# Sums of squares of a recurrence: one fp32 matmul for each half against two fp32r matmuls on high and low parts

## The reference, cut to what matters

```python
qkv_a = jax.nn.silu(causal_conv(qkv_a, conv_w)).astype(jnp.float32)
q_a = qkv_a[..., :GDN_WIDTH].reshape(b, s, GDN_HEADS, GDN_HEAD_DIM)       # 16 heads of 128
k_a = qkv_a[..., GDN_WIDTH:2 * GDN_WIDTH].reshape(b, s, GDN_HEADS, GDN_HEAD_DIM)

def l2norm(x):
    return x * lax.rsqrt(jnp.sum(x * x, axis=-1, keepdims=True) + L2_EPS)
q_a = l2norm(q_a) * (GDN_HEAD_DIM ** -0.5)
k_a = l2norm(k_a)
o_a = gated_delta_rule(q_a, k_a, v_a, g, beta)
```

## Time and profile before

| | |
|---|---|
| median of 3 runs | 3941.32 us (3936.63 to 3944.15) |
| span of the profiled execution | 3936.2 us |
| TensorE matmul / weight load busy | 96% / 91% of the span |
| VectorE busy | 71% |
| ScalarE busy | 48% |
| mean granted TensorE clock | 0.992 |

### The profile page before, as it was taken

How to read it: one execution, slowest core, us unless ns; L and a number is a source line. 1 busy time by engine, 2 the same in 40 slices (tenths; PEclk the granted TensorE clock), 3 DMA queues, 4 the chain that set the end, 5 groups by cost and what they waited for, 6 DMA issues and landing times.

```text
span 3936.2 us, 73085 instructions
## 1 busy us (share of the span) xinstructions
PE 3791.8 (96%) x28822; PEld 3598.6 (91%) x28822; DVE 2786.2 (71%) x3780; ACT 1888.4 (48%) x2849; POOL 185.9 (5%) x188
## 2 busy tenths in 40 slices
PE   1999999999999999999999999999999999999998
PEld 1999999999999999999999999999988798989888
DVE  7788887757777778888675675565576666666676
ACT  1546455335544355555533554454565433334365
POOL 0111211000000012121000000000000000000000
PEclk8999999999999999999999999999999999999999
DMA  9533433863368843434385434445534445555543
GB/s 396 182 141 138 143 135 141 304 220 142 140 236 311 297 148 139 144 138 147 139 317 198 140 140 169 182 162 179 187 111 168 171 171 193 182 183 183 182 149 129
DMA packets 137169, 716.41 MB, mean 182 GB/s; under 512 B 37184, under 2 KB 37632, under 8 KB 60800
## 3 DMA queue, kind: packets, MB, share of 16 engines
q1 hardware_dynamic: 111456, 631.31, 44.6%
q10 hardware_dynamic: 25504, 82.13, 5.9%
HBM read 711.22 MB, written 2.16 MB: 181 GB/s over the span
## 4 chain that ended last, share of the span: by engine, by line
PE 84%; DVE 7%; ACT 4%; issue 3%; DMA 2%; DVEq 0%; ACTq 0%; SPq 0%
PE bank L278 17%; PE bank L280 17%; PE bank L279 17%; PE bank L295 8%; PE bank L296 4%; PE bank L2346 2%; PE bank L2348 2%; PE bank L317 2%; PE bank L2347 2%; ACT Wh L343 2%; PE bank L321 2%; DMA raw<-in_ada 1%; DVE Wl L349 1%; PE bank L319 1%; PE bank L320 1%
## 5 line engine op out<-in xcount | busy, mean ns | idle before, releaser
L343 ACT CAST Wh<-raw 128x1024 fp32r<-128x1024 f32 x1124 | 1169.1, 1047 | 1664.1 <-PE bank L280 1226.0
L349 DVE TENSOR_TENSOR Wl<-raw,Wh 128x1024 fp32r<-128x1024 f32 x1124 | 1383.0, 1235 | 788.9 <-ACT Wh L343 784.1
L278 PE MATMUL bank<-H,Wh 128*128 128x256 f32 x5440 | 1597.0, 294 | 2.0 <-DVE Wl L349 1.2
L279 PE MATMUL bank<-H,Wh 128*128 128x256 f32 x5440 | 1538.4, 283 | 0.0
L280 PE MATMUL bank<-H,Wl 128*128 128x256 f32 x5440 | 1538.0, 283 | 0.0
L278 PEld LDWEIGHTS bank<-H,Wh 128*128 128x128 f32 x5440 | 1041.9, 192 | 29.2 <-issue 17.5
L279 PEld LDWEIGHTS bank<-H,Wh 128*128 128x128 f32 x5440 | 1042.5, 192 | 11.3 <-issue 8.6
L280 PEld LDWEIGHTS bank<-H,Wl 128*128 128x128 f32 x5440 | 1041.5, 191 | 0.0
L295 PE MATMUL bank<-H,Wh 128*128 128x512 f32 x1280 | 449.9, 396 | 6.4 <-DVE WS L336 6.1
L296 PE MATMUL bank<-H,Wl 128*128 128x256 f32 x1280 | 358.6, 280 | 0.0
L295 PEld LDWEIGHTS bank<-H,Wh 128*128 128x128 f32 x1280 | 240.6, 188 | 66.2 <-issue 5.5
(11 more groups left out here) (413 smaller groups left out, 4776.7 us busy)
## 6 DMA issues: line engine op xcount, KB each, us to landing
raw<-in_stream SPq DMA_DIRECT2D x560, 1024.0 KB, 4.8
WS<-in_ada ACTq DMA_DIRECT2D x94, 512.0 KB, 6.1
raw<-in_ada SPq DMA_DIRECT2D x32, 1024.0 KB, 7.6
gm_more<-in_ada ACTq DMA_DIRECT2D x20, 512.0 KB, 6.9
WS<-rows_d ACTq DMA_DIRECT2D x16, 512.0 KB, 5.2
KR<-in_ada ACTq DMA_DIRECT2D x14, 512.0 KB, 6.9
raw<-in_stream SPq DMA_DIRECT2D x8, 512.0 KB, 6.8
X<-in_x_t SPq DMA_DIRECT2D x1, 2048.0 KB, 17.0
```

The costliest lines, as they stand in the source:

```text
L278: pe.matmul(out[:, 0:T], wh, xh[:, kt, :], start=first, stop=False)
L279: pe.matmul(out[:, 0:T], wh, xl[:, kt, :], start=False, stop=False)
L343: act.copy(Wh[:, n % 4, :], raw[:, (sbk + 2) % 4, k * (D // 2):(k + 1) * (D // 2)]).then_inc(hi_ready, 1)
L349: dve.tensor_tensor(Wl[:, n % 4, :], raw[:, (sbk + 2) % 4, k * (D // 2):(k + 1) * (D // 2)], Wh[:, n % 4, :].bitcast(F32), ALU.subtract).t ...
```

## The change

```diff
+        ones_r = sb("ones_r", [P, P], F32R)
...
+        sq_hi, sq_lo = ([O[:, at + h, :, :] for h in range(2)] for at in (KT - 2, KT - 4))
...
             S.done(act.activation(ROPE[:, 1, :], rx[:, 3, :], ACT.Sin), "act", "sin")
+            S.done(act.copy(ones_r[:], ones), "act", "ones_r")
...
                 if n == (SCAN + 4 if chain else SCAN + 3):
-                    F.wait(pe, "act", "sq", f)
+                    if not chain:
+                        st_setup.wait(pe, "act", "ones_r")
+                    F.wait(pe, "dve", "sq_lo1", f)
                     for h in range(2):
-                        m = pe.matmul(B[h][:, :], ones, tm2[:, 2 * h:2 * h + 2, :], start=True, stop=True)
+                        pe.matmul(B[h][:, :], ones_r[:], sq_hi[h], start=True, stop=False)
+                        m = pe.matmul(B[h][:, :], ones_r[:], sq_lo[h], start=False, stop=True)
                     F.done(m, "pe", "ssq")
...
                 if n == (SCAN + 3 if chain else SCAN + 2):
                     F.wait(act, "dve", "silu", f)
+                    for h in range(2):
+                        F.done(act.activation(sq_hi[h], cs2[:, 2 * h:2 * h + 2, :], ACT.Square), "act", f"sq_hi{h}")
                     F.done(act.activation(tm2, cs2, ACT.Square), "act", "sq")
...
+                if fresh and n == (SCAN + 4 if chain else SCAN + 3):
+                    F.wait(dve, "act", "sq", f)
+                    for h in range(2):
+                        F.done(dve.tensor_tensor(sq_lo[h], tm2[:, 2 * h:2 * h + 2, :], sq_hi[h].bitcast(F32), ALU.subtract), "dve", f"sq_lo{h}")
                 if n or not chain:
                     late = 1 if chain else 0
                     dve_low(dve, q + (n - late) // 8, (n - late) // 2 % 4, (n - late) % 2)
```

## The result

The changed kernel takes 3950.03 us (median of 20 runs, 3944.02 to 3955.99), the kernel before 3944.49 us beside it (20 runs, 3936.63 to 3950.11). The ratio is 1.0014, with a 95% interval of 1.0007 to 1.0020: slower by 5.5 us (2.8 to 7.9), and within 0.2%. The forecast was +6.0 us, 3947.3, with a range of 3938 to 3954. It held, though it was put on a median of 3941.3 and the one measured here is 3944.5, and its terms are off by more than the sum shows.

A forecast was written before the change was run, and what follows sets the result against it. The prediction took TensorE's stream and its waits to bound the kernel. Gains of 4.6 us beside chains, losses of 7.6 in first pairs and 3.0 for the clock gave +6.0 on 3941.3: 3947.3 us, range 3938 to 3954.

The forecast's parts named there:

- What is removed and added on TensorE: Sums in each front: two fp32 matmuls (1.72 us) become four fp32r (0.92 us), 0.80 us less to stream.
- The wait beside a chain: In the 14 fronts beside a chain, TensorE waits 0.47 us for VectorE's subtractions before the sums.
- The 14 gains: Each front beside a chain gains 0.80 - 0.47 = 0.33 us, 4.6 us for 14.
- What hides the rest: Beside a chain, idle time on ScalarE (0.51 us) and VectorE (0.75 us) absorbs the delay, so "qkn" moves forward with TensorE.
- The rival that it gives the gain back: At the next chain TensorE waits for "qkn", losing the 14 fronts' gain: +8.8 to +10.6 us, 3951; chance 0.12.
- The wait in the first pairs: In each layer's first pair, without a chain, sums start 4.6 us later; each loses 3.8 us, both 7.6.
- The clock: After each first pair's long wait, TensorE's clock is low for 3.4 us, costing 1.5 us each, 3.0 in all.
- the case of 6.8 us: Rival: the low clock lasts twice as long in both first pairs, +9.0 us, 3950.3; chance 0.09.
- The sum: Whole kernel: -4.6 + 7.6 + 3.0 = +6.0 us, 3947.3 from a median of 3941.3.

The follow-up runs named there:

- e2_wait_only: Changed kernel with its added work and wait kept, but TensorE sums the full squares in fp32 as before; ratio 1.0043 to the kernel before.
- e7_high_only: Changed kernel without full squares and subtractions, TensorE summing only the rounded squares in fp32r at the same place; ratio 0.9972 to the kernel before.
- e3_busy_wait: Changed kernel plus 9 unread fp32 matmuls on TensorE ahead of the long wait in each layer's first pair; ratio 1.0004 to the kernel before.
- e1_first_old: Changed kernel with each layer's first pair back to two fp32 matmuls waiting for the squares alone; ratio 0.9987 to the kernel before.

## Why the prediction was right, point by point

- **What is removed and added on TensorE**: right. 1.72 us before, steps of 0.23 to 0.24 now, 0.80 between e2_wait_only and the changed kernel. For the sustained 131 ns of the Trainium skill ("TensorE: Matmul & The Clock Gate", Back-to-back issue gap) no run here gives a sign; the measured step of 0.23 to 0.24 us stays near its isolated figure.
- **The wait beside a chain**: right in mechanism, 0.41 instead of 0.47. VectorE started the subtractions at 2.48 us after the first square where I had 2.52, and the pair took 1.29 to the end. The 14 gains were put at 4.6 us and came to 5.0.
- **What hides the rest**: right. ScalarE's 0.51 and VectorE's 0.75 of idle time took the delay, and "qkn" kept its distance. The rival that it gives the gain back did not come true; e7_high_only shows where it would have: the wait for "qkn" appears some 0.4 us further on.
- **The wait in the first pairs**: right. 4.72 and 4.58 us where the working had 4.6 from stream to stream. Without the clock (e3_busy_wait) the two pairs lose 3.66 and 3.67 against a forecast of 3.8 each, so 7.3 instead of 7.6 us.
- **The clock**: it did fall in both waits, and e3_busy_wait shows the idle engine as the cause. This term was the one mis-sized most. I took "3.4 us of it with a stream of 256 columns" and 3.0 us in all. It was low for 6.8 us each time, from inside the wait on; in the first layer from about 177.1 to 184.0 by windows of 1 us, so 4.5 us of it lay behind the restart at 179.46. It cost 2.06 and 2.34, 4.4 us in all. I had the case of 6.8 us as a rival at 0.09, ruled down with the argument that the engine goes back to a dense stream. That argument was wrong, for the clock stayed low for 4.5 us of dense stream; but the rival's price of 3.0 us each was too high, since it put all 6.8 us under the stream.
- **The sum**: +6.0 forecast, +7.0 between the two profiles, +5.5 between the medians. Terms: 7.6, 3.0 and -4.6 forecast; 7.3, 4.4 and -5.0 measured, and 0.3 late in the second layer's first pair that no term stands for. A loss too large by 0.3 and a gain too small by 0.4 stood against a clock term too small by 1.4, so that the total came so near is in part luck.

## What to carry to other kernels

Splitting an fp32 sum into two fp32r passes pays on TensorE (0.80 us for 2 x 512 columns here), but each split puts a rounding, a full copy and a subtraction ahead of the sum; the matmuls have to be moved behind that work in TensorE's order, and then waited 0.4 us at most here, beside a chain not at all. Look at every variant of a loop body by itself: 14 gentle fronts hid two bad ones here, which cost more than the 14 gave. And count a wait of several us on TensorE at more than its length: behind 4.6 to 4.7 us of waiting the lower clock cost another 2.1 to 2.3 here.

## What the runs showed that was not expected

The granted clock also falls in places that the change does not touch, in one execution and not in another. Between the layers, windows of the changed kernel and then of e1_first_old:

```profile
1363.00:1373.00 10.00, 10.00 (x82) 9.79 (x81) 3.02 (x4) 2.09 (x2) 0.00 (x0) 1.00 0.97 196
1415.00:1421.00 6.00, 6.00 (x48) 5.52 (x47) 3.42 (x5) 1.91 (x2) 0.00 (x0) 1.00 0.41 164
```
```profile
1363.00:1373.00 10.00, 10.00 (x53) 9.28 (x54) 2.35 (x3) 1.04 (x1) 0.00 (x0) 0.66 0.90 189
1415.00:1421.00 6.00, 6.00 (x39) 5.97 (x39) 1.22 (x1) 1.72 (x6) 1.04 (x1) 0.72 0.70 264
```

In e1_first_old the last mark of the first layer and the first of the second are 835.94 us apart, 8.0 more than the 827.92 of the kernel before, in a stretch where both programs are the same but for one front; e3_busy_wait has 833.72. These 8.0 us are most of why its one profile showed a span of 3945.5 while its runs had a median of 3940.5; the profiled execution was also the slowest of its twelve. By the two windows the clock was low for 6.8 + 3.4 = 10.2 us, worth at most half of that, 5.1 of the 8.0 us; the rest is open. The first of the two stretches began while TensorE ran 32 matmuls of one column (L801):

```profile
1362.82 4.47 PE L801 MATMUL bank<-C,WS 128*128 128x1 f32 x32
```

The kernel before ran the same 32 from 1360.27 on at a clock of 1.00. What decides between the two was not tried. For a change of a few us the distances inside a profile and the intervals of many runs speak; the span of one profile does not.
